# Context keys and values of the second block projected in native fp32 while the first block's expert loop ends

## The reference, cut to what matters

```
x = layer_norm(ALPHA * x + (1 + gt_f) * ffn, ln2_g, ln2_b)          # the end of block one
h     = rmsnorm(x,   g_pre_mix) * (1 + sc1)      + sh1               # block two, 512 tokens
h_ctx = rmsnorm(ctx, g_pre_mix) * (1 + mod_c[1]) + mod_c[0]          # block two, 256 context rows
k_a, v_a, k_b, v_b, q_a, q_b, g_a, g_b = split_cols(h @ w_in, IN_SPLITS)
parts = split_cols(h_ctx @ w_in[:, :KV_COLS], IN_SPLITS[:4])         # k_ca, v_ca, k_cb, v_cb
```

## Time and profile before

| | us |
|---|---|
| median of 3 runs | 2806.41 (2805.61 to 2806.79) |
| the profiled execution | 2807.36 |
| its span (first to last instruction) | 2805.6 |
| last matmul of the e1 loop ends | 790.2 |
| ending: DVE and ACT, until | 833.8 |
| in2: first to last PE work | 835.3 to 1072 |

### The profile page before, as it was taken

The page is one execution under the profiler, slowest core; times in us unless marked ns, Lnnn a source line. Parts: engine busy times, 40 slices in busy tenths (PEclk is TensorE's granted clock), DMA queues, the critical chain, the costliest instruction groups (busy, mean ns, idle before and its releaser), DMA issues. The chain is left out here.

```text
span 2805.6 us, 35430 instructions
## 1 busy us (share of the span) xinstructions
PE 2499.6 (89%) x11924; PEld 2015.0 (72%) x11924; DVE 2177.8 (78%) x2111; ACT 1598.8 (57%) x1492; POOL 469.8 (17%) x330
## 2 busy tenths in 40 slices
PE   6987776999929997877967999999999999999994
PEld 6843665787728896767755778788878888878883
DVE  6787765999954414878556999999999999999995
ACT  3224624777745324556213776777777777777773
POOL 1212002222200000000002112222222222222220
PEclk9998977999969998989976999999999999999997
DMA  8765206999943420020316999999999999999995
GB/s 321 256 213 182 57 30 239 355 370 379 382 148 94 135 73 1 1 91 11 113 42 221 353 372 362 362 366 360 364 361 360 357 362 369 370 368 364 363 361 183
DMA packets 247216, 706.32 MB, mean 252 GB/s; under 512 B 34922, under 2 KB 62841, under 8 KB 244895
## 3 DMA queue, kind: packets, MB, share of 16 engines
q1 hardware_dynamic: 220932, 635.03, 61.7%
q0 software_dynamic: 22240, 59.81, 7.8%
q10 hardware_dynamic: 3968, 10.49, 1.0%
HBM read 686.31 MB, written 41.49 MB: 259 GB/s over the span
## 5 line engine op out<-in xcount | busy, mean ns | idle before, releaser
L50 PE MATMUL psum_all<-sb_ring_r,sb_arena_r 128*128 128x512 f32 (+1 forms) x2400 | 923.4, 385 | 0.0
L158 DVE TENSOR_TENSOR sb_ring_r<-sb_ring,sb_hi_ring 128x2048 fp32r<-128x2048 f32 x285 | 644.6, 2286 | 158.8 <-ACT sb_hi_ring L149 152.3
L158 DVE TENSOR_TENSOR sb_ring_r<-sb_ring,sb_arena_r 128x2048 fp32r<-128x2048 f32 x258 | 582.5, 2285 | 53.4 <-ACT sb_arena_r L149 53.2
L149 ACT ACTIVATE sb_arena_r<-sb_ring 128x2048 fp32r<-128x2048 f32 x258 | 485.0, 1911 | 213.3 <-DMA sb_ring<-in_w_gu_dram 204.3
L149 ACT ACTIVATE sb_hi_ring<-sb_ring 128x2048 fp32r<-128x2048 f32 x285 | 541.2, 1913 | 100.8 <-DMA sb_ring<-in_w_gu_dram 37.9
L49 PE MATMUL psum_all<-sb_hi_ring,sb_arena_r 128*128 128x512 f32 (+1 forms) x1352 | 512.7, 379 | 17.6 <-DVE sb_ring_r L158 5.2
L50 PEld LDWEIGHTS psum_all<-sb_ring_r,sb_arena_r 128*128 128x128 f32 x2400 | 458.1, 191 | 89.7
L51 PE MATMUL psum_all<-sb_hi_ring,sb_arena_r 128*128 128x512 f32 (+1 forms) x1352 | 507.8, 376 | 0.0
L49 PE MATMUL psum_all<-sb_arena_r 128*128 128x512 f32 x1064 | 430.2, 404 | 7.8 <-DVE sb_arena_r L2291 2.5
L51 PE MATMUL psum_all<-sb_arena_r 128*128 128x512 f32 x1080 | 427.6, 396 | 0.0
L49 PEld LDWEIGHTS psum_all<-sb_hi_ring,sb_arena_r 128*128 128x128 f32 x1352 | 258.5, 191 | 73.9 <-DVE sb_ring_r L158 11.6
(11 more groups left out here) (470 smaller groups left out, 3161.1 us busy)
## 6 DMA issues: line engine op xcount, KB each, us to landing
sb_ring<-in_w_gu_dram SPq DMA_DIRECT2D x272, 1024.0 KB, 6.9
sb_ring<-in_w_dn_dram SPq DMA_DIRECT2D x136, 1024.0 KB, 9.1
sb_ring<-in_w_e_gate_dram SPq DMA_DIRECT2D x36, 1024.0 KB, 7.5
sb_ring<-in_w_e_up_dram SPq DMA_DIRECT2D x36, 1024.0 KB, 7.7
sb_ring<-in_w_e_down_dram SPq DMA_DIRECT2D x36, 1024.0 KB, 7.1
sb_ring<-in_w_in_dram SPq DMA_DIRECT2D x27, 1024.0 KB, 6.3
sb_arena<-in_w_ada_dram POOLq DMA_DIRECT2D x32, 512.0 KB, 5.8
sb_ring<-in_w_mod_dram SPq DMA_DIRECT2D x16, 1024.0 KB, 5.4
```

What stands on the lines that cost most here:

```text
L50: eng.matmul(out, a[0], b[1], start=False, stop=False)
L149: act.activation(s.hi[c % len(s.hi)], s.raw[c % len(s.raw)], ACT.Copy).then_inc(s.hi_made, 1)
L158: dve.tensor_tensor(s.lo[c % len(s.lo)], s.raw[c % len(s.raw)], s.hi[c % len(s.hi)].bitcast(F32), ALU.subtract).then_inc(s.lo_made, 1)
```

## The change

- `context_tiles` (new) names the buffers, the five weight chunks that hold context columns and the ten outputs. The outputs are the same places in SBUF as before.
- in r1, SP loads `ctx` first; ACT squares its two tiles (between its two exponentials), DVE forms the mean square and inverts (before it waits for the ranks), ACT takes the root, scales, and, when PE has turned the 16 tiles (before the slot matmuls), applies scale and shift to eight tiles of 256 columns into `con.turned`. No halves are made.
- in the ending of e1, PE gets a program: 10 tiles of 8 plain fp32 matmuls of 256 columns, in four PSUM banks. SP waits for the last matmul of the loop and issues the first two chunks into the high ring's slots, then waits for `finished`, issues the eight y tiles, three more chunks, and the two chunks ahead of in2. ACT empties the ten tiles (`empty(m)`), one at a time between the steps of its hand-written order.
- in in2 everything of the context goes: load, statistics, transposes, halves, and the second uses of five chunks.

```diff
@@ route
         def _(sp):
+            if con is not None:
+                sp.dma_start(con.rows, con.src).then_inc(s.con_landed, 16)
...
@@ route, tensor, between ranks and slot matmuls
+            if con is not None:
+                for t in range(TC):
+                    pe.wait_ge(s.con_scaled, t + 1)
+                    for kk in range(KD):
+                        ins = pe.transpose(k.psum[:, CONTEXT_BANKS[kk // 2], kk % 2 * CTX + t * P:kk % 2 * CTX + (t + 1) * P],
+                                           con.rows[:, t, kk * P:(kk + 1) * P], k.ident[:])
+                ins.then_inc(s.con_turned, 1)
@@ route, scalar
                 act.activation(g_shift, g_shift, ACT.Exp).then_inc(s.gexp, 1)
+            if con is not None:
+                act.wait_ge(s.con_landed, 16)
+                for t in range(TC):
+                    act.activation(con.junk[:, t, :], con.rows[:, t, :], ACT.Square,
+                                   accum_out=con.squares[:, t:t + 1]).then_inc(s.con_squared, 1)
             act.wait_ge(s.wexp_in, 1)
             act.activation(shifted, shifted, ACT.Exp).then_inc(s.wexp, 1)
+            if con is not None:
+                act.wait_ge(s.con_ready, 1)
+                act.activation(con.rstd, con.inv, ACT.Sqrt).then_inc(s.con_root, 1)
+                act.wait_ge(s.con_root, 1)
+                for t in range(TC):
+                    act.activation(con.rows[:, t, :], con.rows[:, t, :], ACT.Copy,
+                                   scale=con.rstd[:, t:t + 1]).then_inc(s.con_scaled, 1)
+                act.wait_ge(s.con_turned, 1)
+                for kk in range(KD):
+                    act.activation(con.turned[:, kk, :], k.psum[:, CONTEXT_BANKS[kk // 2], kk % 2 * CTX:kk % 2 * CTX + CTX],
+                                   ACT.Identity, bias=k.mod["shc"][:, kk:kk + 1], scale=k.mod["scc"][:, kk:kk + 1])
@@ route, vector, after the weights
+            if con is not None:
+                dve.wait_ge(s.con_squared, TC)
+                link(dve.tensor_scalar(con.inv, con.squares, 1.0 / D, 1e-6, ALU.mult, ALU.add))
+                dve.reciprocal(con.inv, con.inv).then_inc(s.con_ready, 1)
             dve.wait_ge(s.ranked, 1)
@@ experts, tensor
             down(n - 1, -nB, PER, n)
+            then.tensor(pe)
@@ combine_and_normalise
+    def tensor(pe):
+        m = 0
+        for i, (_, kind) in enumerate(con.chunks):
+            w = con.weights[i].rearrange("p (a b) -> p a b", b=256)
+            pe.wait_ge(landed_w[i], 16)
+            for half in range(2):
+                if m >= 4:
+                    pe.wait_ge(c.emptied, m - 3)
+                for kk in range(KD):
+                    if kind == "F":
+                        lhs, rhs = w[:, kk, half * P:(half + 1) * P], con.turned[:, kk, :]
+                    else:
+                        lhs, rhs = con.turned[:, kk, half * P:(half + 1) * P], w[:, kk, :]
+                    ins = pe.matmul(bank(m), lhs, rhs, start=kk == 0, stop=kk == KD - 1)
+                ins.then_inc(c.multiplied, 1)
+                m += 1
...
-        sp.wait_ge(finished, 1)
-        rows_of(0)
...
+        sp.wait_ge(chunk_used, chunks + offset)
+        for i, (src, _) in enumerate(con.chunks):
+            if i == 2:
+                sp.wait_ge(finished, 1)
+                rows_of(0)
...
+            sp.dma_start(con.weights[i].rearrange("p (a b) -> p a b", b=256), src).then_inc(landed_w[i], 16)
...
+        def empty(m):
+            act.wait_ge(c.multiplied, m + 1)
+            act.activation(con.outs[m], bank(m), ACT.Copy).then_inc(c.emptied, 1)
         weigh(0)
         weigh(1)
         spread(0)
+        empty(0)
         weigh(2)
         spread(1)
         root(0)
+        empty(1)
         weigh(3)
         square(0)
+        empty(2)
         spread(2)
         root(1)
         square(1)
         apply(0)
+        empty(3)
         spread(3)
         root(2)
+        empty(4)
         square(2)
         apply(1)
+        empty(5)
         root(3)
         square(3)
         apply(2)
+        empty(6)
         apply(3)
+        for m in range(7, len(con.outs)):
+            empty(m)
@@ context_tiles
+    c.weights = [k.hi_plain[:, i, :] for i in range(HI_SLOTS)] + [k.arena[:, 12288 + CHUNK * i:12288 + CHUNK * (i + 1)] for i in range(2)]
...
+    for h in range(2):
+        c.chunks.append((column_chunk(w, 256 * h), "F"))
+        c.outs += [ka[:, 2 * h + i, T:KEYS] for i in range(2)]
+    c.chunks.append((column_chunk(w, 2 * DA), "T"))
+    c.outs += [kvb[:, TT + i, :] for i in range(2)]
+    for h in range(2):
+        c.chunks.append((column_chunk(w, DA + 256 * h), "T"))
+        c.outs += [va[:, TT + i, 256 * h:256 * h + 256] for i in range(2)]
@@ second_in, scalar
             make_hi(act, k, ss, 1)
-            act.wait_ge(s.ctx_ready, 1)
-            act.activation(rstd, inv, ACT.Sqrt).then_inc(s.ctx_root, 1)
             make_hi(act, k, ss, 2)
...
-                if n == CTX_TURN:
-                    act.wait_ge(s.u_lo, KD)
-                    for bank in range(4):
-                        put_ctx(bank)
@@ second_in, vector
-            normalise_ctx()
             make_lo(dve, k, ss, 1)
-            scale_ctx()
             make_lo(dve, k, ss, 2)
@@ block_two_mixer
-    chunks.append((first_kb, [use_t(kvb, 0, 0, u, T), use_t(kvb, TT, 0, uc, CTX)]))
+    chunks.append((first_kb, [use_t(kvb, 0, 0, u, T)]))
...
-        chunks.append((256 * h, [use_f(ka, 2 * h, 0, u, T), use_f(ka, 2 * h, T, uc, CTX)]))
+        chunks.append((256 * h, [use_f(ka, 2 * h, 0, u, T)]))
...
-        chunks.append((DA + 256 * h, [use_t(va, 0, 256 * h, u, T), use_t(va, TT, 256 * h, uc, CTX)]))
+        chunks.append((DA + 256 * h, [use_t(va, 0, 256 * h, u, T)]))
```

More of the change, by code:

```diff
@@ L1928, in first_chunks @@
     return (up_chunks(m, e, m.gate) + up_chunks(m, e, m.up))[0:chunks_ahead(m)]
-Experts = namedtuple("Experts", "width experts top gate up down row_view bias down_bias swiglu whole x y")
+Experts = namedtuple("Experts", "width experts top gate up down row_view bias down_bias swiglu whole x y context")
 def experts(nc, k, name, m, ending):
@@ L1995, in experts @@
         ss.ahead, ss.ahead_landed = chunks_ahead(m), R.ahead_landed
-        then = ending(nc, s.finished)
+        then = ending(nc, s.finished, ss.chunk_used, FIRST)
         block = ctx.enter_context(nc.Block())
@@ L2033, in _ @@
             down(expert(n - 1), -nB, PER, n)
-            then.sync(sp)
+            then.sync(sp, PER * n)
         @block.gpsimd
@@ L2401, in combine_and_normalise, with bank, sync @@
     landed_y = [nc.alloc_semaphore(name=f"cx_y{i}") for i in range(2 * TT)]
-    def sync(sp):
+    c = sems(nc, None, "ck", "multiplied", "emptied")
+    landed_w = [nc.alloc_semaphore(name=f"ck_w{i}") for i in range(len(con.chunks))]
+    def bank(m):
+        return k.psum[:, m % 4, 0:256]
+    def tensor(pe):
[14 more added lines that the diff above has]
+                m += 1
+    def sync(sp, chunks):
         def rows_of(t):
@@ L2511, in combine_and_normalise, with combine_and_store @@
     then = Parts()
-    then.sync, then.scalar, then.vector = sync, scalar, vector
+    then.sync, then.tensor, then.scalar, then.vector = sync, tensor, scalar, vector
     return then
-def combine_and_store(nc, k, y, gain_dram, gate_dram, out, finished):
+def combine_and_store(nc, k, y, gain_dram, gate_dram, out, finished, *rest):
     R = k.route
@@ L2694, in staging, with second_in @@
     return k.rows[:, (i % 4) // 2, 512 * (i % 2):512 * (i % 2) + 512]
-def second_in(nc, k, a, xn, u, uc, ctx_x, ctx_n, chunks, qb, kb, tables, ahead):
+def second_in(nc, k, a, xn, u, chunks, qb, kb, tables, ahead):
     outs = []
@@ L3335, in block_two_mixer @@
     q_heads = qb.rearrange("p t (h d) -> p t h d", d=HD)
[L3336 removed]
+    second_in(nc, k, a, xn, u, [dict(src=column_chunk(w, c), uses=uses) for c, uses in chunks],
               q_heads, kb, tables, len(IN2_FIRST))
@@ L3366, in block_two_moe @@
                 row_view="a (k p) n -> p (a k) n", bias=[a["b_gu_2"][0], a["b_dn_2"][0]], down_bias=2048, swiglu=True,
-                whole=(), x=k.xn_dram, y=k.y_dram)
+                whole=(), x=k.xn_dram, y=k.y_dram, context=None)
     route(nc, k, "r2", 32, 4, 0, m)
-    experts(nc, k, "e2", m, lambda nc, finished: combine_and_store(
-        nc, k, k.y_dram, a["g_post_ffn_2"][0], k.gate_rows[3], out[0], finished))
+    experts(nc, k, "e2", m, lambda nc, *loop: combine_and_store(
+        nc, k, k.y_dram, a["g_post_ffn_2"][0], k.gate_rows[3], out[0], *loop))
 def program(nc, a, out):
```

102 lines of the change are left out of this document (31 added, 71 removed).

## The result

The changed kernel takes 2778.61 us (median of 4 runs, 2776.01 to 2780.48) against 2806.6 for the kernel before on the same chip (4 runs, 2805.61 to 2807.26): ratio 0.9901, 95% interval 0.9888 to 0.9913. Two later comparisons gave 2777.36 and 2779.43. The forecast was 2775, with 2767 to 2796 as its range.

A forecast was written before the change was run, and what follows sets the result against it. PE was taken to bound in2's projection, and a DMA-ACT-DVE-ACT chain the ending, where PE idles. Projection -34.7, ending +3.0 and routing 0 gave -31.7 us from 2806.41: forecast 2775 us (2774.7), range 2767 to 2796.

The forecast's parts named there:

- The projection stage: In in2, removing the context's matmuls and transposes, plus a shorter PE gap and a steadier clock, saves 34.7 us.
- The gap's 2.3 us: In in2, PE's 3.74 us wait for chunk 0's first emptying shrinks by 2.3 us without the context statistics.
- The clock's 2.7 us: In in2, a gap of 1.45 us leaves PE's clock up, so the first tile behind it takes 2.7 us less.
- Rival D: In in2, a stall replaces the context work, so the 29.7 us don't come out; no chance of its own.
- PE's pace: In the ending, a native fp32 matmul of 256 columns takes 0.43 us at 2.4 GHz, 80 of them 35 us.
- Rival B: In the ending, exposed weight loads add 19 us to PE, giving 2792 us; chance 0.08.
- The clock: In the ending, PE's clock rises some 5 us after its start, costing 2.5 us; bounds 35 and 70 us of PE work.
- Rival A: In the ending, PE's clock stays at 1.2 GHz, adding 32.6 us there, giving 2804 us; chance 0.14.
- C: In the ending, low clock and exposed weight loads together add 52 us there, total 2824 us; chance 0.05.
- The loads: In the ending, two weight chunks issued ahead of the y rows delay DVE's first add by 1.5 us, range 0 to 4.
- ACT's queue: In the ending, ten emptyings in ACT's order add 0.3 us before root(3), 0.3 before the last apply, 0.9 behind it.
- PE's cover: In the ending, each tile is ready 2 to 12 us before ACT asks for it, so PE's work stays hidden.

The follow-up runs named there:

- experiment 2: The kernel before, with only the context statistics and root moved behind the halves of chunks 1 and 2 and the first emptying: 2801.85 us, ratio 0.9982.
- experiment 1: The kernel before, plus two unused 1 MB loads issued after the loop's last matmul, ahead of the wait for the last scatter: 2809.09 us, ratio 1.0009.
- experiment 5: The changed kernel with all five weight chunks issued behind the y rows, instead of two ahead of the wait for the last scatter: 2785.77 us, ratio 0.9921.

## Why the prediction was right, and where a term was off

- **The projection stage** came out at -34.5 for -34.7. Its parts: in2 without the context (29.7 forecast), and the gap with the clock behind it, 5.0 forecast, which experiment 2 measured by itself as 4.9. The gap's 2.3 us were worked out from rows and came out as they were. The clock's 2.7 us were partly luck: the reason given, that 1.45 us is well under a gap of 2.21 that left the clock up, does not stand, since a gap of 2.2 us let the clock fall in eight of fourteen profiles; and how much the gap of 3.74 cost before depends on the profile, about 1 us less in that of experiment 1. Rival D (the stage shows a stall where the context work was) fell: PE is busy 177.73 of 180 us, and the 2.27 missing are the gap behind the stage.
- **PE's pace** was taken from the earlier trace rows as 0.43 us for 256 columns; it is 0.437. Rival B (weight loads show) fell: PEld is busy 12.03 of 14 us beside a full PE and adds nothing.
- **The clock**, the doubtful term, went the way of the lower bound. The first eight instructions at 0.50 are 0.42 us each, and the clock is 1.00 from about 801.7, 5 us after the start, as forecast. Rival A (0.14), and C with it, needed it to stay. The row at 1490, native fp32 at 0.50 for 14 us, therefore does not speak of fp32 as such. What differs there is the 32 rows of weights and the 512 columns; no run here tried either alone, so why that stretch stayed at 0.50 is open. The Trainium skill, page "TensorE: Matmul & The Clock Gate", section "Part 1: The HAM clock gate", says that activity releases the throttle and names no data type that would not. The changed kernel agrees with it (0.50 up to 801.7, 1.00 behind), and the row at 1490 still does not.
- **The loads** are the term that was mis-sized: +1.5 taken, with 4 as the upper bound, +4.2 measured, and 4.26 in experiment 1. The step that failed is the one that put the rows right behind the two chunks, at 798.5. The chunks were done at about 799.2, but the rows were issued only at 800.27. They wait for the scatter, the scatter is issued 2 us behind the chunks, and beside them it lands in 7.3 us, not in the 3.2 of the earlier trace rows nor the 5.7 of the earlier trace rows. The earlier trace rows should have been the value and not an extra; it would have given +3.5, still 0.7 short. A reason may be that it is the median of a stream that SP's issues keep evenly filled, while here 2 MB are put down at once; no run shows that.
- **ACT's queue** was +0.6 inside the chain and +0.9 behind it; measured +0.55, and the three last cost 0.9 plus 1.24 us of waiting for PE.
- **PE's cover** held for nine of ten tiles. The last tile was forecast 2.5 us early (834 for 836.5) and was 1.2 late, since the third chunk, behind 4 MB of rows that themselves came 4.2 late, let PE start tile 4 at 817.98 and not at 812.5, with a clock that had fallen in the 4.74 us before and cost some 2 us more. The forecast had PE idle there for only 0.5 us (812 to 812.5), so it charged no clock for it.
- **Routing**: 0 forecast, +0.03 measured (0.10 at the slot matmuls, 0.07 of it brought along).

The ending: 4.2 + 0.55 + 2.2 = 7.0 for 3.0. That is the difference between 2774.7 and 2778.6. The forecast of the total was good because the stage terms were; what moves single profiles besides, mostly ahead of routing and by up to 5 us, is not part of the change.

## What to carry to other kernels

Work moved from a stage that an engine bounds into one where it idles costs little, but price its loads first: ask which small transfer on the critical path they are put in front of, and take for that one no less than the time that the trace shows for it in company (here even that, 5.7 us, was under the 7.3 measured). If the data can lie in a place that is already free, load it before the critical transfer, not beside it; that was worth 5 to 6 us here, while putting it behind cost 7 to 8. Where another engine's program waits for the moved work in a fixed order, look at the first such wait as well as at the last (13.2 and 3.1 us in experiment 5). Where one execution differs from the next by 4 us before the changed stages begin, compare a stage's length in the profile and not the totals.

## What the hardware showed beyond that

- A GpSimd memset of 128x7680 f32 (6.51 us) stopped VectorE: operations of 0.61 and 0.47 us stood for 7.05 and 6.91 us. Moved to where VectorE was idle, the fill cost nothing that the stages show. Even the 0.61 us is a wait: in the kernel before, a memset of 128x1024 on GpSimd ends at 408.67 and VectorE's operation at 408.74, and with the long fill they end at 415.14 and 415.21, each time 0.07 us apart (spans on GpSimd are rough). The Trainium skill, page "SBUF — State Buffer", section "Who interferes with whom", has the two engines share a port pair and calls it an exclusive lock; the rows agree for the first operation. The second reads PSUM and only stood behind the first in the same queue, as far as the rows show.
- The last scatter of a loop, in flight with 2 MB of loads issued 2 us ahead of it, took 7.1 to 7.6 us to land in the four profiles that have them, and 3.2 to 3.3 us in the ten that do not.
- Native fp32 matmuls of 128 rows raised PE's clock from 0.50 to 1.00 after some 5 us of work, and kept it there.
- A gap of 2.17 to 2.28 us ahead of `bias_table` let PE's clock fall in eight of fourteen profiles and not in the other six; one of 1.46 us never did, in twelve. A row in which a gap left the clock up is thus no proof that the next one of its length will.
